# Two transformer blocks in float32 on one core: the second projection group opened early, modulation adds spread anew, q and k turned by DMA

## What is computed

```python
# first block
mod = silu(c) @ w_ada + b_ada                 # 2048 -> 6 x 2048
sh1, sc1, ga1, sh2, sc2, ga2 = split(mod, 6)
h = rms_norm(x, g1) * (1 + sc1) + sh1
qa, ka, va, oa, gates, qb, kb, vb = split(h @ w_in)
h_a = mlstm_bidirectional(qa, ka, va, gates + b_gates)   # 4 heads, then norm, sigmoid(oa)
h_b = neighborhood_attention(qb, kb, vb, rpb)            # 8 heads, bias and window from rpb
x = x + ga1 * (concat(h_a, h_b) @ w_out)
x = x + ga2 * conv_glu(rms_norm(x, g2) * (1 + sc2) + sh2)
# second block
qa, ka, va, qb, kb, vb, ga, gb = split(rmsnorm(x) @ w_in_2)
ya = sliding_window_attention(qa, ka, va) @ w_branch_a   # 16 q heads, 4 k/v heads
yb = stick_breaking_attention(qb, kb, vb) @ w_branch_b   # 16 heads
x = x + (sigmoid(ga) * ya + sigmoid(gb) * yb) @ w_out_2
x = x + swiglu(rmsnorm(x)); return rms_norm(x)
```

## Time and profile before

| | us |
|---|---|
| median of 3 runs | 2589.46 (2588.6 to 2595.97) |
| the profiled execution | 2589.96, span 2588.2 |
| TensorE matmuls busy | 2548.1 (98%) |
| VectorE busy | 1674.6 (65%) |
| ScalarE busy | 1293.0 (50%) |
| GpSimd busy | 221.0 (9%) |
| DMA | 587.87 MB, mean 227 GB/s |

### The profile page before, as it was taken

One profiled execution on the slowest core, in us unless ns is written; L12 is line 12 of the kernel. 1 busy time (PEld: TensorE's weight loads), 2 busy tenths in 40 slices (PEclk: granted clock), 3 DMA queues, 4 the chain that ended last, 5 costly groups with the idle time before them and its releaser, 6 DMA issues.

```text
span 2588.2 us, 31525 instructions
## 1 busy us (share of the span) xinstructions
PE 2548.1 (98%) x11502; PEld 2069.2 (80%) x11502; DVE 1674.6 (65%) x1867; ACT 1293.0 (50%) x1620; POOL 221.0 (9%) x269
## 2 busy tenths in 40 slices
PE   6999999999999999999999999999999999999998
PEld 2788888778888888888888877788888888888887
DVE  4988878978777766555544485756655555555454
ACT  3444456445555554444544466654555555554443
POOL 0031132300000000000100032301000000000000
PEclk8999999999999999999999999999999999999999
DMA  9998987968989787676666555466676666676554
GB/s 395 386 333 268 326 260 247 344 222 264 280 256 273 212 222 209 191 210 204 191 205 194 171 144 150 148 194 205 194 218 202 206 200 211 195 215 201 193 194 155
DMA packets 355536, 587.87 MB, mean 227 GB/s; under 512 B 106196, under 2 KB 106572, under 8 KB 354924
## 3 DMA queue, kind: packets, MB, share of 16 engines
q1 hardware_dynamic: 329488, 514.92, 63.6%
q0 software_dynamic: 18928, 69.39, 7.8%
q10 hardware_dynamic: 7020, 2.26, 0.6%
HBM read 563.94 MB, written 2.10 MB: 219 GB/s over the span
## 4 chain that ended last, share of the span: by engine, by line
PE 89%; DMA 5%; DVE 3%; issue 1%; ACT 1%; SPq 0%; POOL 0%; DVEq 0%; ACTq 0%
PE gp L1529 28%; PE gp L1531 28%; PE gp L1530 28%; DMA raw<-in_w_in_dram 2%; DMA proj<-in_w_ada_dram 2%; DVE w_lo L2039 1%; DMA ada_ring<-in_w_ada_dram 1%; DVE ada_sum L2166 0%; DMA raw<-in_w_up_dram 0%; ACT w_hi L891 0%; PE tp L1795 0%; PE tp L1913 0%; PE tp L1785 0%; PE tp L1998 0%; PE tp L1849 0%
## 5 line engine op out<-in xcount | busy, mean ns | idle before, releaser
L2039 DVE TENSOR_TENSOR w_lo<-raw,w_hi 128x1024 fp32r<-128x1024 f32 x872 | 1075.5, 1238 | 778.3 <-ACT w_hi L891 774.4
L891 ACT CAST w_hi<-raw 128x1024 fp32r<-128x1024 f32 x872 | 911.4, 1050 | 970.9 <-PE gp L1531 770.7
L1529 PE MATMUL gp<-w_hi,h_hi 128*128 128x512 f32 x2648 | 1043.9, 394 | 7.8 <-DVE w_lo L2039 7.3
L1531 PE MATMUL gp<-w_hi,h_lo 128*128 128x512 f32 x2648 | 1031.6, 390 | 0.0
L1530 PE MATMUL gp<-w_lo,h_hi 128*128 128x512 f32 x2648 | 1031.1, 389 | 0.0
L1529 PEld LDWEIGHTS gp<-w_hi,h_hi 128*128 128x128 f32 x2648 | 497.4, 188 | 120.6 <-DVE w_lo L2039 13.8
L1531 PEld LDWEIGHTS gp<-w_hi,h_lo 128*128 128x128 f32 x2648 | 497.3, 188 | 105.0
L1530 PEld LDWEIGHTS gp<-w_lo,h_hi 128*128 128x128 f32 x2648 | 497.7, 188 | 100.7 <-issue 0.2
L1529 PE MATMUL gp<-w_hi,a_hi 128*128 128x512 f32 x704 | 274.3, 390 | 0.0
L1530 PE MATMUL gp<-w_lo,a_hi 128*128 128x512 f32 x704 | 273.9, 389 | 0.0
L1531 PE MATMUL gp<-w_hi,a_lo 128*128 128x512 f32 x704 | 273.9, 389 | 0.0
(11 more groups left out here) (328 smaller groups left out, 1412.7 us busy)
## 6 DMA issues: line engine op xcount, KB each, us to landing
raw<-in_w_in_dram SPq DMA_DIRECT2D x248, 512.0 KB, 4.5
raw<-in_w_up_dram SPq DMA_DIRECT2D x176, 512.0 KB, 4.6
raw<-in_w_ffn_in_dram SPq DMA_DIRECT2D x176, 512.0 KB, 4.4
ada_ring<-in_w_ada_dram POOLq DMA_DIRECT2D x128, 512.0 KB, 5.9
raw<-in_w_down_dram SPq DMA_DIRECT2D x88, 512.0 KB, 4.7
raw<-in_w_ffn_down_dram SPq DMA_DIRECT2D x88, 512.0 KB, 4.7
proj<-in_w_ada_dram SPq DMA_DIRECT2D x64, 512.0 KB, 10.4
raw<-in_w_out_dram SPq DMA_DIRECT2D x64, 512.0 KB, 5.3
```

The costliest lines, as they stand in the source:

```text
L891: nc.scalar.copy(w_hi[:, s], raw[:, s]).then_inc(hi_ready, 1)
L1529: mm(o, hi[:, kt0 + kt, ps], w_hi[:, s, k, :], start=n == 0, stop=False)
L1531: return mm(o, lo[:, kt0 + kt, ps], w_hi[:, s, k, :], start=False, stop=n == g.kts - 1)
L2039: V.tensor_tensor(w_lo[:, s], raw[:, s], w_hi[:, s].bitcast(F32), ALU.subtract).then_inc(lo_ready, 1)
```

## The change

Six things are done.

1. A new product `g_open`, two chunks of the second group, is put between `g_in_a0` and `g_in_a1`. Its class orders the 16 blocks as: first half of K of both chunks, then second half of both. The first-half work thus has 32 blocks (`HALF_B`) and not 24; the sums for the second half of `mod` move to blocks 29 and 30. The second group has 32 blocks left.
2. `halves_adds` is 1 for each block up to 27.
3. The rest of the modulation: 3 adds in the opened chunks, 22 in `g_in_a1` (all steps but 4 and 5), 31 in the second group (steps 1 to 31), 12 in `g_in_o` (steps 4 to 15). The gates' product moves behind block 37, the gate steps 1 to 6 into `g_in_a1`, the heads are 7 steps long.
4. The opening: matmuls on constants (`keep_busy`), the first pair's high part straight from PSUM, its float32 form on VectorE, block 0 and 1 by parts.
5. The row adds of `g_out` go from GpSimd to VectorE.
6. q and k of the second block are turned by DMA during `g_in2a`; the 56 transposes and their copies go, and the attention starts at step 1 without the pause in the middle.

```diff
+class OpenGemm(Gemm):
+    def order(self):
+        h = self.nb // 2
+        return [(e, j) for half in range(2) for e in range(2) for j in range(half * h, (half + 1) * h)]
...
+    g_open = gemm(w_in, 2, col0=GATES0 + 4 * HA, kind=OpenGemm)
     g_in_a1 = gemm(w_in, 3 * WA // CW, k0=HK1, kts=HK1)
-    g_in_b = gemm(w_in, 3 * WA // CW, col0=GATES0 + 4 * HA)
+    g_in_b = gemm(w_in, 3 * WA // CW - 2, col0=GATES0 + 4 * HA + 2 * CW)
+    FRONT = ([(g_in_a0, c // 2, c % 2, j) for c in range(g_in_a0.chunks) for j in range(g_in_a0.nb)]
+             + [(g_open, 0, e, j) for e, j in g_open.order()])
+    HALF_B = len(FRONT) - g_open.nb
...
         def halves_adds(b):
-            if b < 4:
-                return 1 if b < 2 else 0
-            return (2 if b % 2 == 0 else 1) if b <= 20 else 0
-        IN_A_ADA = 20
-        IN_B_SKIP = list(range(6)) + [47]
-        IN_B_ADA = [q for q in range(48) if q not in IN_B_SKIP]
-        IN_O_ADA = list(range(9, 16))
+            return 1 if b < 2 * DT - 4 else 0
+        OPEN_ADA = (37, 38, 39)
+        IN_A1_ADA = [q for q in range(24) if q not in (4, 5)]
+        IN_A_ADA = len(OPEN_ADA) + len(IN_A1_ADA)
+        IN_B_ADA = list(range(1, 32))
+        IN_O_ADA = list(range(4, 16))
...
-        SW0 = 7
+        SW0 = 1
         SK0 = SW0 + HS + 5
-        SK1 = SK0 + 9
+        SK1 = SK0
-        ML0, ML_H = 7, 8
+        ML0, ML_H = 7, 7
...  (SP)
+            def turn_qk(i, e, j, first):
+                c_ = 2 * i + e - 1
+                if 0 <= c_ < QK_TURNS and j == 7:
+                    sp.wait_ge(qk_ready, ST * (c_ + 1))
+                    if c_:
+                        sp.wait_ge(qk_joined, 2 * c_)
+                    for t in range(ST):
+                        sp.dma_start_transpose(qk_turn[:, :, t * P:(t + 1) * P],
+                                               qk_planes(t).rearrange("p w n -> p (w n)")).then_inc(qk_turned, 16)
...  (GpSimd)
             pool.wait_ge(mod_ready, 2)
+            nc.gpsimd.memset(wg_hi[:, :, :].bitcast(F32), 0.0).then_inc(wg_clear, 1)
             ada_cols(range(AR))
+            nc.gpsimd.memset(wg_lo[:, :, :].bitcast(F32), 0.0).then_inc(wg_clear, 1)
             link(nc.gpsimd.memset(ga1, 0.0))
...
-            nc.gpsimd.memset(wg_hi[:, :, :].bitcast(F32), 0.0).then_inc(wg_clear, 1)
-            nc.gpsimd.memset(wg_lo[:, :, :].bitcast(F32), 0.0).then_inc(wg_clear, 1)
...
-            p0 = 0
-            for c_ in range(3):
-                p1 = min(sum(q <= 8 * c_ + 11 for q in OUT_ADA) + AR, len(OUT_ADA))
-                ada_mod(range(p0, p1))
-                add_x(g_out, xt1, c_)
-                p0 = p1
+            ada_mod(range(len(OUT_ADA)))
...  (ScalarE)
+                    if kp == 0:
+                        for kt in range(2):
+                            last = nc.scalar.activation(h_hi[:, kt, :], tp[:, 0, kt * S:(kt + 1) * S],
+                                                        ACT.Identity, bias=mod[:, 0, kt:kt + 1],
+                                                        scale=mod[:, 1, kt:kt + 1])
+                        last.then_inc(h_high, 1)
+                        continue
...
+                if 0 <= m < QK_TURNS and j == 1:
+                    act.wait_ge(qk_turned, 16 * ST * (m + 1))
+                    nc.scalar.copy(qk_half(m, 1), qk_turn_half(m, 1)).then_inc(qk_joined, 1)
...  (TensorE)
+                if n in (13, 14):
+                    pe.wait_ge(const_ready, 1)
+                    keep_busy(4)
...
             scale_rows(gp[1][:, 0, :], 0).then_inc(row_summed, 1)
+            keep_busy(3)
             columns(0)
+            keep_busy(2)
             pe.wait_ge(mod_ready, 1)
             transpose_x(0, (3,), 0)
+            keep_busy(2)
...
+            def open_each(i, e, j, first):
+                b = g_open.block(i, e, j)
+                if b == HALF_B - 3:
+                    pe.wait_ge(h_full, 4)
+                    shift_rows(tp[:, 3, :], 1)
+                    scale_rows(tp[:, 3, :], 1).then_inc(row_summed, 1)
+                if b == HALF_B - 2:
+                    pe.wait_ge(row_ready, 2)
+                    shift_bias(1)
+                    columns(1)
+                if b == HALF_B:
+                    pe.wait_ge(mod_ready, 2)
+                    transpose_x(0, (7,), 0)
+                if b == HALF_B + 5:
+                    mlstm(0)
...  (VectorE)
+            for b in range(HALF_B + 4, len(FRONT)):
+                split(*FRONT[b])
+                if b in OPEN_ADA:
+                    ada2(OPEN_ADA.index(b))
...
+            prime(g_in_a1, (0, 1))
+            dve.wait_ge(gates_mm, 1)
+            drain_open(0, 0)
+            prime(g_in_a1, (2, 3))
+            drain_open(0, 1)
...
+            def in_a1_each(i, e, j, first):
+                q = (2 * i + e) * g_in_a1.nb + j
+                if q in IN_A1_ADA:
+                    ada2(len(OPEN_ADA) + IN_A1_ADA.index(q))
+                a1_after(i, e, j, first)
...
-                        if own:
+                        if g is g_out:
                             dve.wait_ge(drained[t], g.chunk0 + c_ + 1)
                             xs = xres[:, t, bass.ds(g.col(i, e), CW)]
                             V.tensor_tensor(xs, xs, buf[:, e, t, :], ALU.add).then_inc(x_final, 1)
...
+                c_ = 2 * i + e - 1
+                if 0 <= c_ < QK_TURNS and j == 4:
+                    for t in range(ST):
+                        dve.wait_ge(drained[t], g_in2a.chunk0 + c_ + 1)
...
+                            last = V.tensor_copy(qk_planes(t), qk_rows(c_, t))
+                        last.then_inc(qk_ready, 1)
```

More of the change, by code:

```diff
@@ L634, in _ @@
                 load(g_in_a0, 0, 1, j)
[L635 to L638, removed]
-                    load(g, c_ // 2, c_ % 2, j)
+            for b in range(-1, len(FRONT)):
+                if 4 <= b < len(FRONT) - RING:
+                    load(*FRONT[b + RING])
+                elif b >= 4:
+                    load(g_in_a1, 0, 0, b + RING - len(FRONT))
                 for _ in range(4 if b < 0 else halves_adds(b)):
@@ L1045, in drain_half @@
                                    ).then_inc(drained[t], 1)
-            for c_ in range(g_in_a0.chunks):
-                for j in range(g_in_a0.nb):
-                    if c_:
-                        split(g_in_a0, c_ // 2, c_ % 2, j)
-                    if c_ and j == 3:
-                        drain_half((c_ - 1) // 2, (c_ - 1) % 2)
-            prime(g_in_a1, (0, 1))
+            for b, (g, i, e, j) in enumerate(FRONT[:HALF_B]):
+                if b >= RING:
+                    split(g, i, e, j)
+                c_ = b // RING - 1
+                if 0 <= c_ < g_in_a0.chunks and b % RING == 3:
+                    drain_half(c_ // 2, c_ % 2)
+            split(*FRONT[HALF_B])
+            split(*FRONT[HALF_B + 1])
             act.wait_ge(row_summed, 2)
@@ L1203, in drain_o, with in_o_each @@
                                          ).then_inc(drained[t], 1)
-            stream(g_in_o, drain_o, each=at(g_in_o, neighbours), nxt=g_out, unrolled=True)
+            na_at = at(g_in_o, neighbours)
+            def in_o_each(i, e, j, first):
+                if first and j == 1:
+                    mlstm(heads_end + 1)
+                na_at(i, e, j, first)
+            stream(g_in_o, drain_o, each=in_o_each, nxt=g_out, unrolled=True)
             def nothing(i, e):
@@ L1549, in parts, with opened @@
                     last.then_inc(block_used, 1)
+                def opened():
+                    for e, j in g.order():
+                        if j == 0:
+                            for t in range(ST):
+                                pe.wait_ge(drained[t], g.chunk(0, e) - 1)
+                        pe.wait_ge(lo_ready, g.block(0, e, j) + 1)
+                        ready(j)
+                        for k in range(KB):
+                            for t in range(ST):
+                                last = products(e, j, k, t)
+                        last.then_inc(block_used, 1)
+                        each(0, e, j, False)
+                if g is g_open:
+                    return opened()
                 def step(i, e, first):
@@ L2266, in drain_rest, with at @@
                                     ).then_inc(drained[t], 1)
[L2267 to L2269 removed]
+            def at(g, part, k0=0, k1=64):
                 def hook(i, e, j, first):
[L2272 to L2273 removed]
+                    k = (2 * i + e) * g.nb + j - LAG + k0
+                    if (k > k0 if k0 else k >= 0) and k < k1:
                         part(k)
@@ L2436, in drain @@
                         chunk_done(g, i, e)
-                        if c_ >= 2:
+                        if c_ >= 2 and g is not g_out:
                             dve.wait_ge(x_final, done0 + 2 * (c_ - 1))
```

273 lines of the change are left out of this document (137 added, 136 removed).

## The result

The changed kernel takes **2601.97 us** (median of six runs, 2599.13 to 2604.11) against 2589.36 (six runs, 2588.41 to 2595.97): ratio 1.0041, 95% interval 1.0031 to 1.0051, so 8 to 13 us slower. Timed again beside the last experiments the ratio was 1.0051 (1.0037 to 1.0065), at the same median of 2601.97. The profiled execution took 2599.13, its span 2597.4 against 2588.2.

What follows compares the result with a forecast made beforehand. TensorE's own queue was taken as the bound, matmuls being 84% of the chain of waits. Terms -2.0 +9.1 +11.3 +1.5 -6.2 = +13.7 gave 2603.7 us profiled, 2603 against the median; range 2587 to 2611.

Steps and rivals of the forecast that it cites:

- the forecast one: Whole kernel: stalls in the second half of K and the gate-output product, 2603 us against the median, chance 0.58.
- Opening: Before block 4: VectorE's longer queue starts it at 71.4 instead of 69.89 us, +1.5; earlier first products costed at nothing.
- First half of K: First-half-of-K product: 4.1 us of stall goes, 1.5 for block 4 and 0.7 for block 5 come, -2.0 (0 to -4).
- Second half of K: Its start: four adds in a row, late seventh weights and gate steps stall TensorE, +9.1 (+3 to +10).
- Gate-output product: Step 7's modulation weights, requested only behind bias window 7, hold VectorE and then TensorE's score matmul, +11.3 (+7.3 to 14).
- Clock: Behind the gate-output stall: three microseconds of dense work at half rate, +1.5 (0 to 3.4).
- Output product: Row adds move from GpSimd to VectorE, which has time to spare: 0 (-2 to +4).
- Turn of q, k: Second block: 56 transposes leave TensorE, 14 groups at 0.45 us each, -6.2 (-5 to -8).
- the first (the respread holds throughout): Rival: VectorE's lead covers both the gate-output and second-half-of-K stalls, 2581 us, chance 0.14.
- The second: Rival: only the stall behind the bias windows, gate chain's steps absorbed but for 1 us, 2595 us, chance 0.12.
- third: Rival: only the stall in the second half of K, if the windows' biases come early enough, 2590 us, chance 0.08.

Runs made afterwards that it cites:

- the run with the row adds back: Changed kernel with the row adds of the output product's first three chunks back on GpSimd: 2603.47 us, ratio 1.0059.
- the two runs that mended one place each: Changed kernel with GpSimd's gate-output weight requests moved between bias windows: 2590.28 us; changed kernel with second-half-of-K additions on steps 2 to 23: 2597.85 us.
- the run that skips steps 0 and 1: Changed kernel with the 22 additions of the second half of K on steps 2 to 23, not 0 to 3 and 6 to 23: 2597.85 us.
- the run with all three mended: Changed kernel with additions respread in both stalled products, opening additions two blocks later, half windows 0 and 1 in the second group: 2581.57 us, ratio 0.9966.
- requests between the windows: Changed kernel with GpSimd asking for gate-output weights of steps 7 to 11 between bias windows 4 to 7, not behind window 7: 2590.28 us, ratio 0.9999.

## Why the prediction was right, step by step

The time came out at 2601.97 for 2603, and the case was the forecast one. By its terms, against the profiled execution:

- **Opening** (+1.5 for block 4): the mechanism was right, block 4 waited for VectorE's additions. It started at 72.22, not 71.4: 2.3 late. The small gain at block 0 (55.76 against 56.93) was lost there, as said.
- **First half of K** (-2.0): the pairwise stalls are gone, TensorE waits for nothing from 76 to 131 us. But all that lies ahead of the gate-output product, without the 7.1 of the next term, comes to -0.5. The late start of block 4 was mis-sized by 0.8, and the fall of the clock behind it was not counted: it made block 4 take 4.4 us and not 2.7, so 1.7. The 0.7 for block 5 did not come.
- **Second half of K** (+9.1): 7.1. The transfer of the seventh weights was taken at 6.3 us; it took 3.9, and VectorE waited 1.85 and not 4.2. TensorE's longest wait was 2.9 us and not 5.2. The clock fell behind it and cost nothing, by the run with the row adds back. The runs split the 7.1 into 3.2 for additions moved out of the burst (73.39 to 70.14), 3.2 for additions among the gates' steps (70.14 to 66.91) and 0.6 that stays. The last blocks of this stretch differ by 0.7 between profiles, so each part is good to that much.
- **Gate-output product** (+11.3, and +1.5 for the clock behind it): 11.0 together, for 12.8. TensorE waited 8.3 us, since the transfer landed 3.9 us after its request and not 5.8 and VectorE stood 11.7 us, not 14. The 4.6 us at half clock make 2.3 of the rest, inside the range given for it but above its 1.5, which came from three microseconds of dense work at half speed that no row of the kernel before shows (dense blocks ran so from 56.93 to 59.00).
- **Clock** (one fall forecast): three falls in the profiled execution. One cost nothing, so about 4 us of the 5.7 on TensorE reach the time. The Trainium skill's rule ("TensorE: Matmul & The Clock Gate", Part 1), that an array left idle falls back to half clock, was cited for a fall that no row of the kernel before showed. The three rows above show it, behind stalls of 3.2, 2.9 and 8.3 us, and agree with it; but behind the same stall of 2.9 to 3.0 us in the second half of K the clock fell in three profiles out of five. It fell behind all seven stalls of 8.1 to 8.5 us in these runs.
- **Output product** (0): +0.3, and no effect by experiment. **Turn of q, k** (-6.2): -7.0, 0.50 us a group and not 0.45, with nothing given back.

The sum was 2603.7 for a profiled execution, and the one profiled took 2599.1. The second half of K came out 2.0 under its term and the gate-output product with its clock 1.8 under; ahead of them 1.5 were missing; the turn gave 0.8 more. Another 2.0 are the feed-forward's first product, which no term had; the output product and the last one took back 0.7. So errors of both signs met, and that the median, 3 us above the profiled execution, lies 1 us from the forecast is luck; that it is slower by two stalls at the places named is not. Two of the prediction's own sums are off by 0.1, its terms giving +11.4 where it has +11.3 and -1.9 where it has -2.0; together they cancel. Of the rivals, the first (the respread holds throughout) fell by both stalls. The second and third, one stall without the other, are near enough the two runs that mended one place each: 2590.3 where the rival with that stall gone said 2590, and 2597.9 (half the other stall gone) where it said 2595 for nearly all of it.

The change holds the q, k turn, which pays 6 to 7 us, and a schedule whose two stalls cost 18. With the schedule mended it is 9 us faster than the kernel before: in its profile 7.0 from the turn and 2.6 up to the end of the output product, with a feed-forward that took 2.7 longer, inside the spread named above.

## What to carry to other kernels

When work is spread over steps by a list of numbers, follow each item's *request* as well as its use: what stands ahead of it on the queue that issues it, and what that waits for. A request for another engine's next weights belongs ahead of anything on its queue that can block. And give a stall of TensorE a term for the clock behind it, but ask who is late in the blocks that follow: here half clock cost about 2 us behind the stall of 8.3 us, and nothing where VectorE held the next blocks anyway.

## What was not expected of the hardware

**The opening's transfers run at two rates.** In ten of twelve profiles the core moved 418 or 419 GB/s between 15 and 51 us; in two, of unrelated edits, 376 and 387, with the DMA as busy, and the first product started at 60.3 and 60.0 instead of 55.1 to 57.0. The changed kernel's repeat and the run that skips steps 0 and 1:

```profile
15.00:51.00 36.00, 23.79 (x91) 7.27 (x91) 16.84 (x19) 7.72 (x20) 0.00 (x0) 0.72 1.02 418
```

```profile
15.00:51.00 36.00, 22.64 (x69) 5.91 (x70) 14.99 (x18) 7.72 (x20) 0.00 (x0) 0.81 1.03 376
```

So one profile's stretches, not its total, are what an edit is read by. Why the rate differs stays open. The feed-forward's first product takes 482.3 to 487.5 us with the same instructions. TensorE waits 0.6 to 3.8 us there for low halves, and in the two longest cases one wait of about 3 us has half clock behind it, as in the run with all three mended:

```profile
576.70:580.70 4.00, 3.96 (x10) 3.14 (x11) 4.00 (x4) 3.04 (x3) 0.53 (x1) 0.57 0.70 186
```

Why that wait comes in some executions and not in others stays open as well.

**The same opening, and the clock falls in another place.** Up to the gate-output product the changed kernel and the one with requests between the windows are the same program, and TensorE waits 1.8 us ahead of block 2 in both. In the one the clock fell behind that wait, in the other it held until the 3.2 us ahead of block 4. The three microseconds from 66 us, requests between the windows and then the changed kernel:

```profile
66.00:69.00 3.00, 3.00 (x9) 2.34 (x9) 3.00 (x4) 1.05 (x1) 0.00 (x0) 0.61 1.05 405
```

```profile
66.00:69.00 3.00, 3.00 (x14) 2.18 (x12) 3.00 (x4) 1.30 (x2) 0.00 (x0) 1.00 1.05 404
```

Their first-half-of-K stretches are 73.85 and 75.26 us: a fall inside blocks that VectorE holds back anyway is partly hidden, one behind the last stall of the opening is not.
